# A new table of steps for the last stage: dense blocks over 103 U steps, later ones ending ahead of the last U row, diagonals behind the gelu's exponential, two final norms earlier

## What is computed

```python
xn = rmsnorm(h, norm_ffn)
q  = xn @ w_query                        # 8 heads, 2 halves of 128
# per head: top 16 of 128 keys in each half, top 16 of the 256 sums -> 16 experts and gates
u   = expert_u[idx]                      # 128 experts a token, rows of 1024 floats
act = gelu(einsum('ced,cd->ce', u, xn))
out = einsum('ce,ced->cd', gates * act, expert_v[idx])
h   = h + out
y   = rmsnorm(h, norm_final)
```

## Time and profile before

| | us |
|---|---|
| median of three runs | 2223.11 |
| the profiled execution, its own time | 2220.38 |
| its span in the profile | 2218.6 |
| PE busy | 2005.2 (90%) |
| DVE busy | 1204.4 (54%) |
| POOL busy | 895.7 (40%) |
| ACT busy | 424.1 (19%) |
| moved by DMA | 613.48 MB |

### The profile page before, as it was taken

How to read it: one execution, slowest core, us unless ns; L and a number is a source line. 1 busy time by engine, 2 the same in 40 slices (tenths; PEclk the granted TensorE clock), 3 DMA queues, 4 the chain that set the end, 5 groups by cost and what they waited for, 6 DMA issues and landing times.

```text
span 2218.6 us, 24044 instructions
## 1 busy us (share of the span) xinstructions
PE 2005.2 (90%) x9031; PEld 1302.6 (59%) x9031; DVE 1204.4 (54%) x3046; ACT 424.1 (19%) x979; POOL 895.7 (40%) x785
## 2 busy tenths in 40 slices
PE   8999999989989989999888488899998889999996
PEld 7577886755875777786657376544444443333332
DVE  0122100011975778786657999977747775444311
ACT  2233110111212344211111122100003321111001
POOL 0000000000654333453334746666536776666643
PEclk9999999999989999999999757899999999999999
DMA  7422343433898777799868968799988999999996
GB/s 237 133 76 95 118 153 128 147 105 109 325 366 307 235 243 248 251 383 352 284 215 290 343 193 269 269 409 409 409 330 305 352 357 396 409 409 409 409 351 233
DMA packets 252440, 613.48 MB, mean 277 GB/s; under 512 B 18676, under 2 KB 121124, under 8 KB 252324
## 3 DMA queue, kind: packets, MB, share of 16 engines
q0 software_dynamic: 110592, 402.70, 49.3%
q1 hardware_dynamic: 141120, 208.17, 26.9%
q10 hardware_dynamic: 612, 1.07, 0.2%
HBM read 609.77 MB, written 2.10 MB: 276 GB/s over the span
## 4 chain that ended last, share of the span: by engine, by line
PE 68%; DVE 11%; DMA 10%; POOL 5%; issue 3%; ACT 2%; SPq 0%; DVEq 0%; POOLq 0%; ACTq 0%
PE ps L527 28%; PE ps L738 16%; PE ps L539 9%; DMA v_rows<-in_peer_v_dram,idx_turned 6%; PE ps L701 6%; DVE u_rows L1198 4%; POOL v_rows L501 3%; PE ps L564 2%; POOL u_rows L490 2%; PE ps L576 2%; DVE hot_a L1252 2%; PE ps L550 2%; DMA wring<-in_w_branch_attn_dram 1%; PE ps L728 1%; DVE hot_b L1260 1%
## 5 line engine op out<-in xcount | busy, mean ns | idle before, releaser
L490 POOL DMA_INDIRECT u_rows<-in_peer_u_dram,idx x512 | 600.9, 1174 | 1105.8 <-DVE idx L1185 563.3
L1198 DVE CUSTOM_DVE_ANT_0 u_rows<-u_rows,xn 128x1024 f32<-128x1024 f32 x512 | 619.6, 1217 | 185.7 <-DMA u_rows<-in_peer_u_dram,idx 183.7
L527 PE MATMUL ps<-xT,wring 128*128 128x256 f32 x2560 | 578.6, 386 | 10.7 <-DVE xT L992 4.8
L527 PEld LDWEIGHTS ps<-xT,wring 128*128 128x128 f32 x2560 | 492.3, 194 | 81.1 <-DVE xT L992 4.8
L738 PE MATMUL ps<-d_rows,gates 128*128 128x512 f32 x1024 | 455.2, 598 | 0.0
L738 PEld LDWEIGHTS ps<-d_rows,gates 128*128 128x128 f32 x1024 | 190.0, 190 | 265.2 <-issue 265.2
L701 PE MATMUL ps<-v_rows,diag 64*64 64x512 f32 x2048 | 264.3, 636 | 42.7 <-DMA v_rows<-in_peer_v_dram,idx_turned 40.7
L501 POOL DMA_INDIRECT v_rows<-in_peer_v_dram,idx x128 | 150.1, 1173 | 159.9 <-PE ps L701 131.5
L728 PEld LDWEIGHTS ps<-hot_b,hot_a 128*128 128x128 f32 x1024 | 149.9, 233 | 69.4 <-DVE hot_b L1260 42.6
L728 PE MATMUL ps<-hot_b,hot_a 128*128 128x64 f32 x1024 | 158.7, 322 | 31.1 <-DVE hot_b L1260 30.9
L701 PEld LDWEIGHTS ps<-v_rows,diag 64*64 64x64 f32 x2048 | 74.1, 139 | 191.2 <-issue 161.9
(11 more groups left out here) (167 smaller groups left out, 1780.6 us busy)
## 6 DMA issues: line engine op xcount, KB each, us to landing
wring<-in_w_in_dram SPq DMA_DIRECT2D x128, 512.0 KB, 6.2
d_rows<-in_peer_v_dram SPq DMA_DIRECT2D x128, 512.0 KB
wring<-in_peer_w_query_dram SPq DMA_DIRECT2D x32, 512.0 KB, 6.6
wring<-in_w_branch_conv_dram SPq DMA_DIRECT2D x16, 512.0 KB, 6.3
wring<-in_w_branch_attn_dram SPq DMA_DIRECT2D x16, 512.0 KB, 4.6
wring<-in_w_out_dram SPq DMA_DIRECT2D x16, 512.0 KB, 4.8
wring<-in_xattn_wq_dram SPq DMA_DIRECT2D x16, 512.0 KB, 4.6
wring<-in_xattn_wo_dram SPq DMA_DIRECT2D x16, 512.0 KB, 5.7
```

The lines of the kernel that those rows point to most:

```text
L490: pool.indirect_dma_start(out=u_rows[:, n % URING, :], out_offset=None, in_=peer_u[0], in_offset=bass.IndirectOffsetOnAxis(ap=experts_of(g ...
L527: mm = pe.matmul(bank(job)[:, 0:HN], w[:, k % 4, P * b:P * (b + 1)], act[:, k, :], start=(k == 0), stop=(k == KT - 1))
L1198: dve.tensor_tensor_reduce(out=u, in0=u, in1=(xn2 if h else xn1)[:, i, :], scale=1.0, scalar=0.0, op0=ALU.mult, op1=ALU.add, accum_out=dot ...
```

## The change

All three tables change, and with them the places of a few steps:

```diff
-    CH_SLOT = spread(12, 46, 32) + spread(142, 170, 32)
-    BLK_SLOT = spread(48, 140, 64) + spread(171, 264, 64)
-    V_SLOT = spread(24, 46, 22) + spread(48, 141, 14) + spread(142, 170, 88) + spread(171, 280, 132)
-    V_AHEAD, DIAG_AHEAD = 4, 2
-    END = V_SLOT[-1] + 1
-    ADD_SLOT = HSTEPS + 141
+    CH_SLOT = spread(12, 46, 32) + spread(153, 179, 32)
+    BLK_SLOT = spread(48, 151, 64) + spread(181, 253, 64)
+    V_SLOT = spread(24, 46, 22) + spread(48, 152, 14) + spread(153, 179, 82) + spread(181, 280, 138)
+    V_AHEAD, DIAG_AHEAD, DIAG_BEHIND = 4, 2, 4
+    END = V_SLOT[-1] + DIAG_BEHIND + 1
+    ADD_SLOT = HSTEPS + 152
+    LAST_ADD, LAST_NORMS = STEPS + 9, STEPS + 18
...
-        DIAG_OF.setdefault(slot - DIAG_AHEAD, []).append(m)
+        DIAG_OF.setdefault(slot + (DIAG_BEHIND if slot >= BLK_SLOT[64] else -DIAG_AHEAD), []).append(m)
...
-            for t in (0, 1, 3):
-                finish_norm(t)
+                if tau == LAST_NORMS:
+                    finish_norm(0)
+                    finish_norm(1)
+            finish_norm(3)
...
-            add_dense(1)
+                if tau == LAST_ADD:
+                    add_dense(1)
+            finish(0)
+            finish(1)
             add_experts(1)
-            for t in (0, 1, 3):
-                finish(t)
+            finish(3)
```

## The result

The changed kernel takes 2231.36 us (median of 12 runs, 2226.55 to 2238.55) against 2223.03 us of the kernel before in the same rounds (12 runs, 2219.0 to 2228.68). The ratio is 1.0036, 95% interval 1.0022 to 1.0050: slower by 8.3 us. The forecast was 2230.6, 7.5 us slower.

The account below looks back on a forecast made before the run. PE was taken to bound both dense parts, with DMA nearly full. Terms -3.3 - 13.5 - 7 + 32.3 - 1 sum to +7.5 us, giving 2230.6 us against the median of 2223.11; range 2218 to 2240.

Parts of the forecast that it names:

- What bounds the kernel: Last stage: PE bounds both dense parts; reordering removes no PE work, only changes some 45 us of idle time.
- Second dense part, -13.5 and -7: Seven fewer pairs and four fewer block-pair changes save 13.5 us of PE time; sooner V rows save 7 us idle.
- Tail, +32.3: After the last dense block: ten more pairs at 3.23 us each, set by a ring of three pairs, add 32.3 us.
- Middle part, -3.3: Eight fewer POOL issues save 12.3 us, less 9 us lost in front by late V rows: -3.3 us.
- Now it stands behind U row 148, which needs dot 142: First dense part: V row 35, queued behind U row 148, issues at 1628.5, lands at 1644.5; PE stands 7 us.
- If pair 17 doesn't wait: Sign that the forecast is wrong: PE was to stand some 7 us for V row 35 near 1637.
- Diagonals, 0: Second dense part: moving the diagonals costs 0 us, bounds 0 and +5.
- End, -1: End of the kernel: less traffic before the last output saves 1 us, bounds -0.4 and -2.
- Rival B: Tail at POOL's pace, 2.48 us a pair if landings are short: 2218.6 us; chance 0.13, with C 0.08.
- Rival C: Middle part: V rows 35 to 37 land in time, saving 12.3 us: 2221.6 us; chance 0.19 together with E.
- Rival D: Tail: granted clock falls for every late pair, +7.2 us, 2237.8 us in all; chance 0.12.
- Rival E: Whole stage: transfers alone set the time whatever the order, so it stays 2223 us; chance 0.19 together with C.

Follow-up runs that it names:

- e2: Changed kernel with V rows 36 to 39 issued with U row 149 instead of behind U row 157: 2233.49 us, ratio 1.0054 to the kernel before.
- e3: Changed kernel with V rows from 216 on using a ring of 14 places (eight of `u_rows`, six of `v_rows`): 2208.12 us, ratio 0.9939.
- e8: Changed kernel with the end of the change undone (additions, norms and finishes as before): ratio 1.0033 to the kernel before.
- e9: Changed kernel with all diagonals two steps ahead of their slot again: ratio 1.0033 to the kernel before.
- e7: Kernel before with a ring of 14 places for V rows from 228 on, all tables as they were: ratio 0.9945.
- e12: e10 with V rows 36 to 39 issued with U row 149, as in e2: ratio 0.9950 to the kernel before.
- e6: Kernel before with only the end of the change (last additions, norms and order of finishes): ratio 1.0004.
- e10: Changed kernel with second dense blocks up to step 262 and a ring of 14 for V rows from 216 on: ratio 0.9921 to the kernel before.
- e1: Changed kernel with second dense blocks ending at step 262 as before, tail of 12 pairs instead of 20: 2220.33 us, ratio 0.9987 to the kernel before.
- e4: Kernel before with second dense blocks ending at step 251 instead of 262, tail of 17 pairs instead of 10: 2222.65 us, ratio 0.9990.
- e11: e4 with the ring of 14 places, for V rows from 228 on: ratio 0.9966 to the kernel before.

## Why the prediction was right, step by step

- **What bounds the kernel**: right. In both dense parts PE is the bound, and PE's work in the stage didn't change (749.0 us busy in the earlier trace rows, 750.5 in the windows above).
- **Second dense part, -13.5 and -7**: measured -20.5, to the tenth by luck, since e2, e3, e8 and e9, with the same blocks and pairs, gave 325 to 330 us.
- **Tail, +32.3**: measured +34.2. The step "at the tail's own spacing" assumed 3.23 us; it was 3.36, with the clock at 0.92. The mechanism, three pairs in the ring, is shown by e3 and e7: with more places the waits shrink or go.
- **Middle part, -3.3**: right within what can be read (-0.9 with the first dense part), but by a wrong step. "Now it stands behind U row 148, which needs dot 142" is wrong: `u_rows` has eight places, not six as the text on the kernel says, so U row 148 needs dot 140. V row 35 went out at 1624.48 instead of 1628.5, landed in time, and PE did not stand for 7 us; PE's idle time in the first dense part is 0.5. "If pair 17 doesn't wait" was one of the prediction's own signs of being wrong, and it came true. The sum didn't hang on it, since pair 18 waits for V row 37 with or without it: the second step there, pair 18 and V row 42 about 9 us late, did come about. But the 9 us which the sum takes for it were mostly not lost: the late start alone was undone in e2 and e12 without a gain. And over all profiles the first dense and middle part together take 413.7 us in the mean with the changed tables (nine, 407.9 to 419.9) and 419.9 with those of before (five, 413.6 to 426.9), 6 us less and not 3.3; the spread is wider than that difference.
- **Diagonals, 0**: right (e9). **End, -1**: 0.7 in the profile, nothing in the medians (e6, e8).
- **Rival B**, the tail at POOL's pace, did not happen by itself: the shortest landing was 4.4 us in the changed kernel's tail too. Its 2.5 us a pair is what the ring of 14 brings about, with a landing of over 8 us. I had tied it to a short landing; the number of places serves as well. The fit of the Trainium skill ("DMA: Bandwidth & Descriptors", the anatomy of a SWDGE DMA) gives, by my estimate, 3.2 us for a V row. The shortest landing of one that the traces of the last stage hold is 4.2 us (e2), so the traces disagree with it.
- **Rival C**: its 2221.6 did not come, and its condition didn't either, since V row 37 was late. e2 brings the condition about, and still no 9 us came back.
- **Rival D**, the falling clock, came in part. The changed kernel's tail had 0.92, e2's 0.83, and 1.00 never appears in the tails of 12 pairs or more with a ring of six. The Trainium skill, "TensorE: Matmul & The Clock Gate", the part on the HAM clock gate, says that an idle window halves the clock. The trace agrees in so far as e3, e7 and e10, whose tails idle 8.8 of 45.6, 0.2 of 18.6 and 2.3 of 25.8 us, kept 1.00, and the changed kernel's, idle 22.5 of 64.3 us, did not; but the tail before idled 11.0 of 30.1 us and kept 1.00 too. In the changed kernel it costs at most about 2 us, if all of the wider spacing is its doing (53.7 us for 16 spacings where 3.23 would give 51.7), less than the 7.2 which I had given for every pair. That the clock is the cause of the wider spacing was not tested by itself.
- **Rival E**, that the order does nothing: refuted. The interval of the ratio, 1.0022 to 1.0050, leaves 1 out, and two parts moved by 20 us and more. e1 and e4, both within 0.2% of before, show how near such moves can come to cancelling.
- **The sum**: the profiles differ by 14.4 us and the medians by 8.3. The two profiled executions account for that: the one of before took 2220.38, 2.7 under its median, the one of the changed kernel 2234.73, 3.4 over its own. The means over all profiles with the same table of a part give -6.2 for the first dense and middle part, -20.8 for the second dense part, +33.5 for the tail and -0.7 for the end, +5.8 in all. So the tail and the second dense part are right in mechanism and size, and the forecast within 1 us of the total is partly luck, since the middle part gave some 3 us more and the tail took 1 to 2 more. In a single profile the middle part can't be read closer than that: it varied from 172 to 184 us under one table.

## What to carry to other kernels

When work is moved out of a part that one engine fills, ask what a unit of it costs where it goes: here 1.9 us between dense blocks and 3.2 in a tail that waits for its own small ring. Before shortening or lengthening such a tail, count the buffers that are idle by then; eight places of another, finished ring took 5 to 19 us off it, and 0.55% off the time of the kernel before, which no table of steps here did. Start them early enough: rows behind one that waits for the small ring come too late (e11). A timeline that shows k items at once and then one wait per item, with the spacing times k equal to release, issue and landing together, is the mark of a ring that is too short.

## What the runs showed of the hardware

- Landing of a 512 KB row gather isn't a constant. At the median it took 16.0 us in the saturated first dense part, 11.5 in the second (9.8 to 14.2 between 1885 and 2110), 5.2 in the tail of before, and 8.1 to 8.6 in e3's tail, where more of them were in flight at 359 GB/s; with POOL issuing one every 1.24 us and the DMA engines at 412 GB/s there, they grew to 9.9 us.
- With the ring of six the mean granted clock of the tail was below 1.00 in all six profiles with tails of 12 pairs or more and in one of the two with 10; with the ring of 14 it was 1.00 in five of six (e11 0.96).
- Three chips gave 2223.1, 2232.35 and 2234.93 us for the same kernel, up to 0.5% apart, more than the change itself.
